# The value projection of two attention groups as seven products each, with strided operands and a weight sum made by an adding transfer

## The chip, the cores and the metric

One core of a Trainium2 chip runs the kernel. The metric is the device time of one execution in microseconds (us); several executions are timed and their median is given. The core has a matrix engine (TensorE, PE in the rows; its loads of a stationary tile are PEld), VectorE (DVE), ScalarE (ACT), GpSimd (POOL) and SyncE (SP). Each runs its own queue of instructions in order, and they wait for each other through semaphores.

## What is computed

The reference is a stack of four transformer layers on 512 tokens of width 1024 in fp32. The change concerns the value part of one of them, a dilated attention with three groups:

```python
proj = (u @ w_in).astype(jnp.float32).reshape(B, S, N_GROUPS, 3, ATT_HEADS, ATT_HEAD_DIM)
for gi, (window, dilation) in enumerate(((128, 1), (512, 4), (2048, 16))):
    q = apply_partial_rope(proj[:, :, gi, 0], cos, sin) * scale
    k = apply_partial_rope(proj[:, :, gi, 1], cos, sin)
    v = proj[:, :, gi, 2]
    o_g, lse_g = dilated_group_attention(q, k, v, window, dilation)
```

For each group `v` is a product of `u` (512 x 1024) with 1024 columns of weights. Groups 1 and 2 use their tokens by residue modulo four, so their rows of `v` are wanted with the tokens of one residue together.

## The kernel before

Matrix products are taken in fp32 precision from two fp32r parts: every operand is split into an upper part (`u_hi`, `w_hi`) and a lower part (`u_lo`, `w_lo`), and three matmuls (`PASSES`: hi x hi, hi x lo, lo x hi) stand for one.

Weights go through the kernel in chunks of 512 rows by 512 columns (four row tiles of 128), numbered in one sequence over the whole kernel. There are three slots (`SLOTS`), so chunk c lies in slot c modulo 3. SyncE loads a chunk into `raw` once chunk c - 3 has been used (`wait_used`, then `chunk`). ScalarE makes its upper part (`split` in its block, line 745), VectorE its lower part (`split` in its block, line 1440), TensorE waits for that with `s_lo`. Both splits run two chunks ahead: while chunk c is being used, `split(name, b, s)` handles c + 2. Each engine's program is a fixed list over `order`, so an instruction that waits holds back everything behind it on its engine.

The value projection is the stage `at_v`: six blocks of 512 weight columns, two chunks each, 96 matmuls of 512 columns a block. In each the stationary tile is 128 tokens of `u` (128 columns) and the moving one is the weights. Block 0 is done in two halves, since it begins while the operand `u` is still being made (`head`, line 2554; lines 1707, 909 and 1719 make the operand from the normed rows, the last of them the lower parts). The blocks of groups 1 and 2 (2 to 5) use copies of `u_hi` and `u_lo` in which the tokens lie by residue; ScalarE (line 1368) and VectorE (line 2267) make these copies during block 1. ScalarE moves each finished tile out of PSUM (line 1363). After the stage VectorE and ScalarE make the tables of the rotary embedding (`rope_tables`). Then the projection of queries and keys follows (`at_qk0`, TensorE's line 2412), whose chunks come in four transfers of 256 KB each.

Late in the kernel, the second product of a feed-forward network is already done as seven products instead of eight, a Strassen-Winograd scheme on 2 x 2 quarters (stages `ff_st`, function `products`, line 2365). Its order of products is A11, A11_21, A2_SUM, A12, A22_21, A22, A_SUM, its weight quarters are loaded by `quadrant_loads` (line 636) in eight transfers of 512 KB, VectorE makes the weight sums (lines 1446, 1455, 1461) and one sum is made by GpSimd's adding transfer (line 724):

```python
pool.wait_ge(s_wsum, 3 * q + 2)
pool.wait_ge(s_lo, c0 + B21 + 1)
pool.dma_start(W21, W11, accum_op=ALU.add).then_inc(s_fourth, 16)
```

VectorE adds each product into the result (`products_added`, line 1478), behind the split of the chunk two further on.

Of the kernel before, what the change touches and what calls it, by code (L numbers as in the profile page):

```python
# [21 lines left out]
P = 128  # L22
S = 512
# [23 lines left out]

A11, A11_21, A12, A22, A22_21, A2_SUM, A_SUM = range(7)
# [96 lines left out]
def gemm_plan():  # L145
# [17 lines left out]
    add("at_v", 6, KT, "act")  # L163
# [15 lines left out]
    c = t = inner = groups = 0  # L179
    freed = {"act": 4, "dve": 4}  # L180
    for name in order:
        g = plan[name]
        if g["evictor"] is None:
            g.update(c0=c, group=groups)
            c += g["chunks"]
            groups += 1
            continue
# [8 lines left out]
def build(nc, a, out, gates, where1, where2, where3, stop=None):  # L196
# [12 lines left out]
    with ctx:  # L209
# [37 lines left out]
        with ExitStack() as room:  # L247
            at_v = sb("at_v", [P, TB, GROUPS * D], F32, room)
            with ExitStack() as sub:
                by_residue_hi, by_residue_lo = sb("u_hi_by_residue", [P, KT, S], F32R, sub), sb("u_lo_by_residue", [P, 4, S], F32R, sub)  # L250
            at_qk = sb("at_qk", [P, 2, 2 * GROUPS, S], F32, room)
# [61 lines left out]
        s_con1, s_cols, s_rows, s_x = sem("constants_and_rope_tables_landed"), sem("columns_landed"), sem("rows_landed"), sem("x_and_masks_landed")  # L313
# [23 lines left out]
        by_residue_lo = [(by_residue_lo if k < 4 else by_residue_in_tmp)[:, k, :] for k in range(KT)]  # L337
        residues = lambda t: t.rearrange("p (c r) -> p r c", r=4)
        by_four = lambda t: t.rearrange("p (r c) -> p r c", r=4)
        s_res_hi, s_res_lo = sem("u_hi_by_residue_ready"), sem("u_lo_by_residue_ready")  # L340
        s_rope1, s_out = sem("first_rope_done"), sem("result_written")
        s_quad = [sem("weights_landed_11_22"), sem("weights_landed_12_21")]
        s_fourth, fourth0 = s_ada[0], 16 * (2 * ADA_BLOCKS - ADA_FIRST)
# [209 lines left out]
        def wait_used(eng, c):  # L553
# [3 lines left out]
            if g["evictor"] is None:  # L557
                eng.wait_ge(s_prod, 14 * g["group"] + 2 * s + 2)
# [54 lines left out]
        def _(sp):  # L613
# [23 lines left out]

            sp.dma_start(con1[:, :], a["con1"]).then_inc(s_con1, 16)
# [16 lines left out]
            for name in order:  # L655
# [16 lines left out]
                if g["evictor"] is None:  # L672
                    continue
# [16 lines left out]
            last = 14 * plan[order[-1]]["group"]  # L690
# [8 lines left out]
        def _(pool):  # L699
# [18 lines left out]
            for name in order:  # L718
                if plan[name]["evictor"] is None:
                    q, c0 = plan[name]["group"], plan[name]["c0"]  # L720

                    pool.wait_ge(s_wsum, 3 * q + 2)
# [5 lines left out]
        def _(act):  # L728
# [3 lines left out]
            def split(name, b, s):  # L732
# [6 lines left out]
                of, _, i = where_chunk[c]  # L739
                if plan[of]["evictor"] is None:  # L740
# [5 lines left out]

            def weights_upper(c, q, i):

                wait_used(act, c - SLOTS)
                if i in (B11, B22, B21):  # L750
                    act.wait_ge(s_quad[1 if i == B21 else 0], 64 * (q + 1))
                elif i == B_SUM4:
                    act.wait_ge(s_fourth, fourth0 + 16 * (q + 1))
                else:
                    act.wait_ge(s_wsum, 3 * q + 1 + (B12_22, B_SUM3, B11_12).index(i))
# [579 lines left out]
            for name in order:  # L1335
# [23 lines left out]
                elif name == "at_v":  # L1359
# [5 lines left out]
                    def upper_by_residue(b):  # L1365
                        if b == 0:
                            for k in range(KT):
                                sc.copy(by_four(by_residue_hi[:, k, :]), residues(u_hi[:, k, :])).then_inc(s_res_hi, 1)
                        if b == 2:
                            gate_rows_out(2, 3)  # L1370
                    linear(name, values, after=upper_by_residue)
# [46 lines left out]
        def _(dve):  # L1418
# [9 lines left out]
            def split(name, b, s):  # L1428
# [5 lines left out]
                of, _, i = where_chunk[c]  # L1434
                if plan[of]["evictor"] is None:
# [5 lines left out]

            def first_sum(q):

                for j in range(2):
                    dve.wait_ge(s_quad[j], 64 * (q + 1))
                tt(W12, W12, W22, ALU.add).then_inc(s_wsum, 1)

            def weights_lower(c, q, i):

                if i == B12_22:  # L1450
                    if q not in FIRST_GROUPS:
                        first_sum(q)
                    dve.wait_ge(s_wsum, 3 * q + 1)
# [4 lines left out]
                if i == B21:  # L1458
                    dve.wait_ge(s_lo, c + 1)
                    dve.wait_ge(s_wsum, 3 * q + 2)  # L1460
                    tt(W12, W11, W22, ALU.subtract).then_inc(s_wsum, 1)

            def products_added(name):
# [5 lines left out]
                for s in range(len(PRODUCTS)):  # L1469
                    if s:  # L1470
                        split(name, 0, s)
                    for t in range(2):
                        dve.wait_ge(s_prod, 14 * q + 2 * s + t + 1)
# [1590 lines left out]
```

## Time and profile before

| what | value |
|---|---|
| median of 3 runs | 2894.68 us (2894.61 to 2895.87) |
| the profiled execution, its own time | 2896.12 us |
| its span in the profile | 2894.3 us |
| TensorE busy with matmuls | 2864.8 us, 99% |
| TensorE busy with weight loads | 2366.1 us, 82% |
| VectorE busy | 1693.6 us, 59% |
| ScalarE busy | 1227.6 us, 42% |
| granted clock, mean | 0.999 |

The span is the time from the first to the last instruction of the profiled execution; the device time has a little around it. Positions in the trace are in us from the start of the span. A matmul's shown duration includes the time in which it fills and drains, so matmuls overlap; what one of them costs in a stream is the distance between two starts.

### The profile page before, as it was taken

Reading aid. Unit: us, or ns where it says so; the run is one execution under the profiler, and the core shown is the slowest. Engines: PE = TensorE matmul, PEld = TensorE weight load, DVE = VectorE, ACT = ScalarE, POOL = GpSimd, SP = SyncE. Lnnn points to the kernel's source line nnn. Section 1 sums busy time; section 2 is a strip of 40 time slices with the busy share of each in tenths; the row PEclk is TensorE's granted clock in tenths of the full one; section 3 lists DMA queues with packets and bytes.
Section 4 is the critical chain, followed back from the end, with each engine's and each line's share of the span. In section 5 each row is a group of like instructions: output and inputs, shape, how many; then the busy total and the mean of one; then the engine's idle time right before and its main releaser. Section 6 shows DMA issues by size and latency. Waiting matters only on the chain.

```text
span 2894.3 us, 38609 instructions
## 1 busy us (share of the span) xinstructions
PE 2864.8 (99%) x16106; PEld 2366.1 (82%) x16106; DVE 1693.6 (59%) x2470; ACT 1227.6 (42%) x1882; POOL 74.0 (3%) x63
## 2 busy tenths in 40 slices
PE   7999999999999999999999999999999999999999
PEld 6878887888887777888888877888888877888887
DVE  6776656645255656533335764666674663656677
ACT  5555422235233333531324465454444455444444
POOL 0000011200000000000000000000000000000000
PEclk9999999999999999999999999999999999999999
DMA  8443355542332222233332222224423222234323
GB/s 303 168 138 117 117 187 184 189 135 91 99 102 65 78 68 77 67 109 95 102 99 84 88 88 74 88 102 131 131 77 106 77 84 73 88 117 131 104 87 115
DMA packets 224637, 320.93 MB, mean 111 GB/s; under 512 B 16496, under 2 KB 123344, under 8 KB 223568
## 3 DMA queue, kind: packets, MB, share of 16 engines
q1 hardware_dynamic: 207504, 266.96, 28.7%
q0 software_dynamic: 11888, 49.29, 5.4%
q10 hardware_dynamic: 5072, 2.23, 0.3%
q8 instruction: 127, 2.08, 0.3%
q14 instruction: 46, 0.38, 0.0%
HBM read 308.98 MB, written 2.11 MB: 107 GB/s over the span
## 4 chain that ended last, share of the span: by engine, by line
PE 89%; DVE 5%; ACT 3%; DMA 2%; issue 1%; ACTq 0%; SPq 0%; DVEq 0%
PE G L2412 46%; PE G L2419 16%; PE G L2471 5%; PE G L2365 4%; PE G L2454 4%; PE X L2365 4%; PE X L2738 1%; PE G L2437 1%; PE X L2516 1%; DMA ada_raw<-in_ada_w 1%; PE X L2752 1%; DVE w_lo L1440 1%; DVE w_lo L1457 1%; DMA raw<-in_w_ff 1%; PE X L2838 1%
## 5 line engine op out<-in xcount | busy, mean ns | idle before, releaser
L2412 PE MATMUL G<-u_hi,w_hi 128*128 128x512 f32 x2096 | 835.0, 398 | 1.9 <-issue 1.9
L2412 PE MATMUL G<-u_hi,w_lo 128*128 128x512 f32 x2096 | 817.6, 390 | 0.0
L2412 PE MATMUL G<-u_lo,w_hi 128*128 128x512 f32 x2096 | 817.0, 390 | 0.0
L1440 DVE TENSOR_TENSOR w_lo<-raw,w_hi 128x2048 fp32r<-128x2048 f32 (+3 forms) x210 | 471.8, 2249 | 437.8 <-ACT w_hi L745 436.7
L745 ACT CAST w_hi<-raw 128x2048 fp32r<-128x2048 f32 (+3 forms) x214 | 401.8, 1878 | 426.1 <-DMA raw<-in_w_ff 148.2
L2412 PEld LDWEIGHTS G<-u_hi,w_hi 128*128 128x128 f32 x2096 | 393.7, 188 | 89.1 <-issue 9.3
L2412 PEld LDWEIGHTS G<-u_hi,w_lo 128*128 128x128 f32 x2096 | 393.5, 188 | 84.1
L2412 PEld LDWEIGHTS G<-u_lo,w_hi 128*128 128x128 f32 x2096 | 394.1, 188 | 78.6 <-issue 1.4
L2252 DVE TENSOR_TENSOR hid_f<-silu_g,G 128x512 f32<-128x512 f32 x44 | 30.1, 688 | 167.2 <-PE G L2412 153.9
L1573 DVE SCALAR_TENSOR_TENSOR acc<-ada_raw,cond,acc 128x512 f32<-128x512 f32 x140 | 105.2, 752 | 13.3 <-DMA ada_raw<-in_ada_w 3.9
L2454 PE MATMUL G<-u_hi,w_hi 128*128 128x256 f32 x384 | 109.3, 285 | 2.8 <-DVE u_lo L1719 2.8
L2454 PE MATMUL G<-u_lo,w_hi 128*128 128x256 f32 x384 | 108.7, 283 | 0.0
L2454 PE MATMUL G<-u_hi,w_lo 128*128 128x256 f32 x384 | 108.6, 283 | 0.0
L2419 PE MATMUL G<-w_hi,hid_hi 128*128 128x512 f32 x256 | 99.7, 389 | 0.6 <-issue 0.6
L2419 PE MATMUL G<-w_lo,hid_hi 128*128 128x512 f32 x256 | 99.6, 389 | 0.0
L2419 PE MATMUL G<-w_hi,hid_lo 128*128 128x512 f32 x256 | 99.6, 389 | 0.0
L2419 PE MATMUL G<-w_hi,u_hi 128*128 128x512 f32 (+1 forms) x256 | 98.2, 384 | 0.0
L2419 PE MATMUL G<-w_lo,u_hi 128*128 128x512 f32 (+1 forms) x256 | 96.5, 377 | 0.0
L2419 PE MATMUL G<-w_hi,u_lo 128*128 128x512 f32 (+1 forms) x256 | 96.4, 377 | 0.0
L1346 ACT ACTIVATE silu_g<-G 128x512 f32<-128x512 f32 x44 | 26.1, 598 | 161.4 <-PE G L2412 152.0
L2365 PE MATMUL G<-w_hi,hidden_sums_hi 128*128 128x512 f32 x224 | 87.2, 389 | 0.0
L2365 PE MATMUL G<-w_hi,hidden_sums_lo 128*128 128x512 f32 x224 | 87.2, 389 | 0.0
(512 smaller groups left out, 4726.3 us busy)
## 6 DMA issues: line engine op xcount, KB each, us to landing
raw<-in_ffn_w_in SPq DMA_DIRECT2D x88, 512.0 KB, 4.8
ada_raw<-in_ada_w POOLq DMA_DIRECT2D x40, 1024.0 KB, 5.7
raw<-in_w_ff SPq DMA_DIRECT2D x72, 512.0 KB, 4.5
raw<-in_w_in SPq DMA_DIRECT2D x56, 512.0 KB, 4.0
raw<-in_attn_w_in SPq DMA_DIRECT2D x96, 256.0 KB, 3.7
raw<-in_ffn_w_out SPq DMA_DIRECT2D x40, 512.0 KB, 4.6
raw<-in_hgrn_w_in SPq DMA_DIRECT2D x32, 512.0 KB, 4.8
yT<-in_w_ff SPq DMA_DIRECT2D x28, 512.0 KB, 8.9
```

The source lines that it names most:

```text
L745: sc.copy(w_hi[slot][:, 0:nk, 0:w], raw[slot][:, 0:nk, 0:w]).then_inc(s_hi, 1)
L1440: tt(w_lo[slot][:, 0:nk, 0:w], raw[slot][:, 0:nk, 0:w], w_hi[slot][:, 0:nk, 0:w].bitcast(F32), ALU.subtract).then_inc(s_lo, 1)
L1457: tt(w_lo[c % SLOTS][:, :, :], weights_of[i], w_hi[c % SLOTS][:, :, :].bitcast(F32), ALU.subtract).then_inc(s_lo, 1)
L1573: ins = stt(acc, ada_raw[:, s, k, :], c, acc, ALU.mult, ALU.add)
L2252: evicted(g, b, 2 + m, lambda: tt(fold(hid_f[:, m, :]), fold(silu_g[:, m, :]), summed_tile(name, b, 2 + m), ALU.mult))
L2365: ins = mm(product_bank(s, t), xs[ix][:, x, k, blk(t)], w[iw][:, k, :], start=s not in order_in_bank and (k, iw, ix) == (0, 0, 0), stop=(k ...
L2412: ins = mm(G[0:c1_ - c0, m, :], w[iw][:, k, c0:c1_], xs[ix][:, x0(b) + kk, :], start=first, stop=last, skip_group_check=True)
L2419: ins = mm(G[:, m, o0:o1], x[:, blk(tok)], w[iw][:, k, c0:c1_], start=first, stop=last, skip_group_check=True)
L2437: ins = mm(G[:, m, :], w[iw][:, k, blk(m)], xs[ix][:, x0(b) + k, :], start=(k, iw, ix) == (0, 0, 0), stop=(k, iw, ix) == (3, 1, 0), skip_g ...
L2454: ins = mm(half_tile(hf, m), w[iw][:, k, m * P:m * P + P], xs[ix][:, kk, half[hf]], start=m % 2 == 0 and kk == 0 and (iw, ix) == (0, 0), s ...
L2471: ins = mm(G[:, j, :], xs[ix][:, kk, blk(j)], w[iw][:, k, :], start=kk == 0 and (iw, ix) == (0, 0), stop=kk == g["ktiles"] - 1 and (iw, ix ...
L2516: ins = tr(turned(k)[:, blk(i)], y[:, 2 * hf + i, blk(k)], ident)
```

## The change

The stage `at_v` keeps two blocks (group 0). Groups 1 and 2 become the stages `at_st0` and `at_st1`, each of seven products. Each product is a 256-token half by a 512-row half of `u` with a 512 x 512 quarter of the weights or a sum of quarters: 2 token tiles x 4 row tiles x 3 passes. The token halves are residues 0 and 1, and residues 2 and 3. Three operands (A11, A12, A22) are read from `u_hi` and `u_lo` with a stride of four tokens; four are sums. Of these VectorE makes the fp32 values (`value_sums`, eight instructions of 1,024 elements a partition), ScalarE the upper parts (`value_sums_upper`) and VectorE the lower parts (`value_sum_lower`). The copies by residue go.

The weight quarters live in the rooms `V11`, `V12` and `V22`; `V12` holds B12, then B21. They are loaded by SyncE (`value_quadrant`, `value_loads`), the first three ahead of the second chunk of block 1. B_SUM4 is made by GpSimd's adding transfer of `V11` onto `V12`; after it VectorE takes `V22` from `V11` for B11_12. The order of products is A11, A11_21, A2_SUM, A12, A22, A22_21, A_SUM, numbered here from 0. Products 0 and 3 are moved out by ScalarE, the others are added or subtracted by VectorE.

```diff
-    add("at_v", 6, KT, "act")
+    add("at_v", 2, KT, "act")
+    for i in range(2):
+        add(f"at_st{i}", 1, KT, None)
...
+        V11, V12, V22 = yT[:, 0:4, :], yT[:, 4:8, :], tmp[:, 0:4, :]
+        value_weights = {B11: V11, B12_22: V12, B_SUM3: V11, B21: V12, B_SUM4: V12, B11_12: V11, B22: V22}
+        VALUE_PRODUCTS, VALUE_WEIGHTS = (A11, A11_21, A2_SUM, A12, A22, A22_21, A_SUM), (B11, B12_22, B_SUM3, B21, B_SUM4, B11_12, B22)
+        by_residue = lambda t, kh, th: t.rearrange("p k (c r) -> p k r c", r=4)[:, 4 * kh:4 * kh + 4, 2 * th:2 * th + 2, :]
...
+            def value_loads(name):
+
+                i, c0 = int(name[-1]), plan[name]["c0"]
+                sp.wait_ge(s_lo, c0 + 2)
+                value_quadrant(i, V12, 1, 0, s_quad[1])
+                if i == 0:
+                    sp.wait_ge(s_lo, c0 + 5)
+                    value_quadrant(1, V12, 0, 1, s_quad[1])
+                    sp.wait_ge(s_lo, c0 + 6)
+                    value_quadrant(1, V11, 0, 0, s_quad[0])
+                    sp.wait_ge(s_lo, c0 + 7)
+                    value_quadrant(1, V22, 1, 1, s_v22)
...
+                        if name == "at_v" and (b, s) == (1, 1):
+
+                            sp.wait_ge(s_u, 6 * KT)
+                            value_quadrant(0, V12, 0, 1, s_quad[1])
+                            value_quadrant(0, V22, 1, 1, s_v22)
+                            value_quadrant(0, V11, 0, 0, s_quad[0])
...
+                if name.startswith("at_st"):
+                    pool.wait_ge(s_wsum, 3 * int(name[-1]) + 2)
+                    pool.wait_ge(s_lo, plan[name]["c0"] + 4)
+                    pool.dma_start(V12, V11, accum_op=ALU.add).then_inc(s_fourth, 16)
...
+            def value_weights_lower(c, q, s):
+
+                x = VALUE_WEIGHTS[s]
+                if x == B12_22:
+                    if q:
+                        first_value_sum(q)
+                    dve.wait_ge(s_wsum, 3 * q + 1)
+                    dve.wait_ge(s_lo, c)
+                    tt(V11, V11, V12, ALU.add).then_inc(s_wsum, 1)
+                elif x == B_SUM4:
+                    dve.wait_ge(s_fourth, fourth0 + 16 * (q + 1))
+                    tt(V11, V11, V22, ALU.subtract).then_inc(s_wsum, 1)
+                dve.wait_ge(s_hi, c + 1)
+                tt(w_lo[c % SLOTS][:, :, :], value_weights[x], w_hi[c % SLOTS][:, :, :].bitcast(F32), ALU.subtract).then_inc(s_lo, 1)
...
+            def value_products_added(name):
+
+                g, i = plan[name], int(name[-1])
+                first, second = (slice((i + 1) * D + 512 * nh, (i + 1) * D + 512 * nh + 512) for nh in range(2))
+                for s in range(len(PRODUCTS)):
+                    split(name, 0, s)
+                    if s in (0, 3):
+                        continue
+                    for t in range(2):
...
                 elif name == "at_v":
...
+                    split(name, 0, 0)
+                    split(name, 0, 1)
+                    first_value_sum(0)
+                    value_sums()
+                    split(name, 1, 0)
+                    value_sum_lower(A11_21, 1)
+                    value_sum_lower(A2_SUM, 0)
+                    split(name, 1, 1)
+                    value_sum_lower(A22_21, 3)
+                    value_sum_lower(A_SUM, 2)
...
+            def value_products(name):
+
+                g, i = plan[name], int(name[-1])
+                for s, x in enumerate(VALUE_PRODUCTS):
+                    pe.wait_ge(s_lo, g["c0"] + s + 1)
+                    slot = (g["c0"] + s) % SLOTS
+                    w, xs = (w_hi[slot], w_lo[slot]), value_operands[x]
+                    if x in VALUE_READY:
+                        pe.wait_ge(s_res_lo, VALUE_READY[x])
+                    for t in range(2):
+                        bank = (G[:, t, :], G[:, 2 + t, :], X[:, t, :], G[:, t, :], G[:, 2 + t, :], X[:, t, :], X[:, t, :])[s]
+                        added = {1: -6 + t + 1, 2: -2 + t + 1, 4: t + 1, 5: 2 + t + 1, 6: 6 + t + 1}.get(s)
...
```

The feed-forward groups keep their work; only the values that their semaphores are counted up to move.

## Rows read from the trace of the kernel before

**Rows 1.** The chain of waits, 690 to 860: start, length, what, matmuls

```profile
699.26 108.80 PE G L2419 x480
808.06 48.96 PE G L2412 x216
```

**Rows 2.** Timeline of VectorE, 676 to 722: start, duration, what, idle before

```profile
692.11 0.42 DVE L1719 TENSOR_TENSOR u_lo<-tmp,u_hi 128x256 fp32r<-128x256 f32 x1 [0.21 <-ACT u_hi L909]
...
701.72 2.29 DVE L1440 TENSOR_TENSOR w_lo<-raw,w_hi 128x2048 fp32r<-128x2048 f32 x1 [5.58 <-ACT w_hi L745]
703.93 2.24 DVE L2267 CAST u_lo_by_residue<-u_lo 128x512 fp32r<-128x512 f32 x4
```

**Rows 3.** Weight loads by line: count, minimum/median/maximum ns, first and last start

```profile
L2738 PEld LDWEIGHTS X<-at_qk x768: 134/138/167, 856.9 to 1168.5; 128*32 128x32 f32 x192
...
L2749 PEld LDWEIGHTS X<-at_v,tmp x512: 101/107/133, 867.4 to 1173.7; 32*32 32x32 f32 x43, 96*32 96x32 f32 x43, 128*32 128x32 f32 x43, 64*32 64x32 f32 x42
...
L2419 PEld LDWEIGHTS G<-w_hi,u_hi_by_residue x128: 187/188/188, 720.6 to 807.0; 128*128 128x128 f32 x128
```

**Rows 4.** Timeline, 1008 to 1012: four packed weight loads in a row

```profile
1010.94 0.52 PEld L2752 LDWEIGHTS X<-at_v,tmp 128*128 128x128 f32 x4 [0.20 <-issue]
```

**Rows 5.** Timeline of ScalarE, 1895 to 1990

```profile
1925.83 1.91 ACT L745 CAST w_hi<-raw 128x2048 fp32r<-128x2048 f32 x1 [0.73 <-DMA raw<-in_w_ff]
...
1967.00 1.91 ACT L756 CAST w_hi<-yT 128x2048 fp32r<-128x2048 f32 x1 [3.34 <-DMA yT<-yT]
...
1977.45 1.91 ACT L745 CAST w_hi<-raw 128x2048 fp32r<-128x2048 f32 x1 [6.72 <-DMA raw<-in_w_ff]
```

**Rows 6.** Groups of VectorE by shape, 690 to 2000: count, busy us, mean ns

```profile
L1633 DVE TENSOR_TENSOR w_lo<-raw,w_hi 128x1024 fp32r<-128x1024 f32 x4 | 4.9, 1216 | 0.0
```

**Rows 7.** Timeline of VectorE, 1895 to 1990

```profile
1957.05 2.28 DVE L1457 TENSOR_TENSOR w_lo<-yT,w_hi 128x2048 fp32r<-128x2048 f32 x1
...
1979.39 2.29 DVE L1440 TENSOR_TENSOR w_lo<-raw,w_hi 128x2048 fp32r<-128x2048 f32 x1 [3.56 <-ACT w_hi L745]
1981.60 1.28 DVE L1478 TENSOR_TENSOR h_by_token<-h_by_token,G 128x512 f32<-128x512 f32 x2
```

**Rows 8.** Timeline of GpSimd, 1880 to 1990

```profile
1959.94 0.93 POOL L724 DMA_DIRECT2D yT<-yT  x1 [1354.10 <-DVE w_lo L1457]
```

**Rows 9.** Timeline of SyncE's transfers, 780 to 830

```profile
786.33 43.89 SPq L621 DMA_DIRECT2D raw<-in_attn_w_in  x17
```

**Rows 10.** Timeline of ScalarE, 783 to 850

```profile
792.73 1.91 ACT L745 CAST w_hi<-raw 128x2048 fp32r<-128x2048 f32 x1 [4.00 <-DMA raw<-in_attn_w_in]
```

**Rows 11.** Timeline of SyncE's transfers, 1880 to 1990

```profile
1907.80 0.88 SPq L636 DMA_DIRECT2D yT<-in_w_ff  x2
...
1916.48 67.71 SPq L625 DMA_DIRECT2D raw<-in_w_ff  x8
```

**Rows 12.** The chain of waits, 1935 to 2000

```profile
1972.41 5.44 PE G L2365 x24
1977.85 5.44 PE X L2365 x24
```

**Rows 13.** Busy us and instructions by stretch, then clock, DMA share, GB/s

```profile
25.00:28.00 3.00, 1.21 (x11) 0.97 (x10) 1.63 (x5) 2.23 (x4) 0.00 (x0) 1.00 1.05 387
28.00:31.00 3.00, 2.80 (x7) 2.25 (x8) 2.46 (x3) 2.97 (x5) 0.00 (x0) 0.57 1.05 387
...
474.00:477.00 3.00, 1.29 (x6) 1.11 (x7) 2.96 (x6) 1.68 (x1) 1.89 (x1) 1.00 0.90 331
```

**Rows 14.** Copies by line: count, minimum/median/maximum ns, first and last start

```profile
L1368 ACT CAST u_hi_by_residue<-u_hi x8: 1118/1124/1132, 701.6 to 708.7; 128x512 fp32r<-128x512 f32 x8
...
L2267 DVE CAST u_lo_by_residue<-u_lo x4: 630/634/644, 703.9 to 705.5; 128x512 fp32r<-128x512 f32 x4
...
L1363 ACT COPY at_v<-G x24: 577/587/593, 693.7 to 808.1; 128x512 f32<-128x512 f32 x24
```

More of the change, by code:

```diff
@@ L183, in gemm_plan @@
         if g["evictor"] is None:
-            g.update(c0=c, group=groups)
+            g.update(c0=c, prod0=prod0, add0=add0)
             c += g["chunks"]
-            groups += 1
+            prod0 += 14
+            if name.startswith("at_st"):
+                g.update(act0=freed["act"])
+                freed["act"] += 4
+                add0 += 10
+            else:
+                g.update(group=groups)
+                groups += 1
+                add0 += 14
             continue
@@ L689, in _ @@
             by_token = out[0].rearrange("(b p) n -> p b n", p=P)
-            last = 14 * plan[order[-1]]["group"]
+            last = plan[order[-1]]["add0"]
             for added, rows, cols in ((10, slice(2, 4), upper_columns), (12, slice(0, 4), lower_columns), (13, slice(0, 1), upper_columns),
@@ L745, in split, with value_weights_upper, value_products_out @@
                 sc.copy(w_hi[slot][:, 0:nk, 0:w], raw[slot][:, 0:nk, 0:w]).then_inc(s_hi, 1)
+            def value_weights_upper(c, q, s):
+                wait_used(act, c - SLOTS)
+                x = VALUE_WEIGHTS[s]
+                if x == B11:
+                    act.wait_ge(s_quad[0], 32 * (q + 1))
+                elif x == B21:
+                    act.wait_ge(s_quad[1], 64 * (q + 1))
+                elif x == B22:
+                    act.wait_ge(s_v22, v22_0 + 32 * (q + 1))
+                elif x == B_SUM4:
+                    act.wait_ge(s_fourth, fourth0 + 16 * (q + 1))
+                else:
+                    act.wait_ge(s_wsum, 3 * q + 1 + (B12_22, B_SUM3, B11_12).index(x))
+                sc.copy(w_hi[c % SLOTS][:, :, :], value_weights[x]).then_inc(s_hi, 1)
+            def value_products_out(name):
+                g, i = plan[name], int(name[-1])
[4 more added lines that the diff above has]
+                        for t in range(2):
+                            act.wait_ge(s_prod, g["prod0"] + 2 * s + t + 1)
+                            if s == 0:
+                                sc.copy(at_v[:, 2 + t, first], G[:, t, :])
+                                ins = sc.activation(at_v[:, t, second], G[:, t, :], ACT.Identity, scale=-1.0)
+                            else:
+                                ins = sc.copy(at_v[:, t, first], G[:, t, :])
+                            ins.then_inc(s_free["act"], 1)
             def weights_upper(c, q, i):
@@ new lines, in value_sums @@
+            def value_sums():
+                hi = lambda kh, th: by_residue(u_hi, kh, th).bitcast(F32)
+                lo = lambda kh, th: by_residue(u_lo, kh, th).bitcast(F32)
+                f11_s2, f21_t1, f12_s4, f22_s1 = value_f
+                n.own(s_u)
+                tt(f11_s2, hi(0, 0), lo(0, 0), ALU.add)
+                tt(f21_t1, hi(0, 1), lo(0, 1), ALU.add)
+                link(tt(f22_s1, hi(1, 1), lo(1, 1), ALU.add))
+                link(tt(f22_s1, f22_s1, f21_t1, ALU.subtract))
+                n.give(tt(f21_t1, f11_s2, f21_t1, ALU.subtract), d2a)
+                ins = stt(f11_s2, f22_s1, -1.0, f11_s2, ALU.mult, ALU.subtract)
+                n.give(ins, d2a)
+                n.own(d2a)
+                link(tt(f12_s4, hi(1, 0), lo(1, 0), ALU.add))
+                n.give(stt(f12_s4, f11_s2, -1.0, f12_s4, ALU.mult, ALU.subtract), d2a)
@@ L2568, in head @@
                                 turn(tail_of[name], 1)
[L2570 removed]
+            after_products = {order[i + 1]: plan[name]["add0"] for i, name in enumerate(order[:-1]) if plan[name]["evictor"] is None}
             tail_of = {b: a_ for a_, b in TAILS.items()}
```

155 lines of the change are left out of this document (113 added, 42 removed).

## Prediction

> **What bounds the kernel now.** Read the chain of waits first. From 699.26 on it is one run of 480 matmuls of line 2419 in 108.80 us, followed without a gap by the projection after it [rows 1]: 226.7 ns a matmul, whatever the other engines do. In the value projection TensorE alone sets the time. VectorE there is idle most of the time, each of its weight subtractions ending a wait for ScalarE [rows 2]. So removed matmuls come back in full, at 0.2267 us each, but only while every weight operand is made before its product begins. That cover is what I read next: the order of the queues and what each step costs.
>
> **The gain.** Four blocks of 96 matmuls (384) become two groups of 7 products x 24 (336). 48 x 0.2267 = 10.9 us less. No later stage changes its work, so what moves is the start of the query and key projection, 808.06 now [rows 1].
>
> **Strided operands on TensorE.** Three products of seven take their stationary tile from every fourth token: 2 x 3 x 24 = 144 loads. The trace has such a load only 32 columns wide: 138 ns against 107 ns for a packed one, so 31 ns per 32 columns. At 128 columns that is 188 + 4 x 31 = 312 ns [rows 3]. The matmul does not wait for the whole of a load: four packed loads in a row take 0.52 us with the last one's 0.19, so 0.11 us each, though one lasts 0.19 [rows 4]. A strided one then needs 0.110 + 0.124 = 0.234 us, against a pitch of 0.227. Bounds: nothing, or 312 - 227 = 85 ns if nothing of the excess overlaps, 0 to 12.2 us over 144. I take 7 ns, 1.0 us, since the packed row shows the overlap.
> The Trainium skill (SBUF — State Buffer, Specifications (TRN2)) says that full bandwidth needs at least two accesses in the same 16-byte line, and that each crossing pays. Fp32 with a stride of four crosses at every element. The trace agrees for the stationary load (138 against 107 ns) and for ScalarE; for VectorE see the rivals.
>
> **Prices of the chain.** ScalarE's upper part of a chunk: 1.9 us [rows 5]. VectorE's lower part or weight sum: 2.2 us from start to start [rows 2]. A sum of 1,024 elements: 1.22, next start after 1.13 [rows 6]. Adding a product: 0.64 each [rows 7]. The adding transfer: VectorE's lower part starts at 1957.05 and ends at 1959.3 [rows 7], GpSimd issues at 1959.94 [rows 8], ScalarE is released at 1967.00 [rows 5]: 7.65 us from end to use. Two weight transfers, 1 MB, in an empty queue: a feed-forward product ends at 1972.41 [rows 12], which lets SyncE issue, and ScalarE is released at 1977.45 [rows 5], 5.04; with the waits 5.1 us. The first half chunk of the next projection (four transfers): issue 786.33 [rows 9], release 792.73 [rows 10], 6.4 us.
>
> **Block 1 of the value projection.** Its second chunk used to be ready at 701.72 + 2.2 = 703.9 [rows 2]; TensorE needs it 432 matmuls ahead of 808.06 [rows 1], at 710.1. Now SyncE first waits for the whole operand (last lower part 692.11 + 0.42 = 692.5 [rows 2]) and issues six 512 KB transfers ahead of the chunk's two. The nearest row: eight such and two more, issued from 1907.80 on [rows 11], release ScalarE at 1925.83 [rows 5], 18.0 us for ten. Less two at 1.3 us (0.39 MB per us): 15.4 us, so 708.0. Upper 1.9, lower 2.2: 712.15. **Stall 2.1 us**; the block ends at 723.0 instead of 721.0. Bounds: none if the chunk lands by 705.6, 4 us if ten transfers' time is needed.
>
> **First group, seven products of 5.44 us** (24 x 0.2267; the strided ones 5.61).
> - Product 0. Behind the late chunk VectorE has in order: the first weight sum (2.2), eight operand sums (8 x 1.13 and about 0.5 for waits on itself, 9.5), then the lower part of B11 (2.2). 712.1 + 13.9 = 726.1. The block ended at 723.0: **stall 3.1**. ScalarE's evictions, behind its casts of these sums, end at about 725.2, under this.
> - Product 1. Two lower parts of operand sums (2.3), the weight sum (2.2), the lower part of B12_22 (2.2): 732.8. Product 0 ends at 731.7: **stall 1.1**.
> - Products 2 and 3 are covered: 737.2 and 742.0 against 738.3 and 743.7.
> - Product 4 needs B_SUM4. B21 can be loaded only after 732.8, into the room of B12: + 5.1 + 1.9 + 2.2 = 742.0. Then the adding transfer 7.65, VectorE's V11 - V22 (2.2), the lower part (2.2): 754.1. Product 3 ends at 749.3: **stall 4.8**. The feed-forward groups take their fourth sum one product later and into a buffer of its own; here one product of cover less is 5.4 us less.
> - Product 6 accumulates in the bank of product 5 and waits for VectorE to have added that. VectorE first serves the split for the next group: B11 of group 2 is loaded after the lower part of B11_12 (754.1, two adds 1.2, 2.2: 757.5): + 5.1 + 1.9 + 2.2 = 766.8, and the add 0.64: 767.5. Product 5 ends at 765.2: **stall 2.3**. It ends at 772.9.
>
> **Second group.** V22 reloads behind the lower part of B22 (759.7) and has landed when VectorE comes to it, behind the adds of product 5, at 768.1. Two weight sums and the lower part of B12_22, 6.6: 774.7, in time for product 1 (778.6). B21, + 9.2 and a wait: 784.0. Adding transfer and two VectorE steps: 796.0, product 3 ends at 795.1: **stall 1.0**. Product 4 ends at 801.7. SyncE's queue holds the first chunk of the next projection behind that end, as its room counter is three chunks back: + 6.4 + 1.9 + 2.2 = 812.2, and VectorE adds product 5 only after it: 812.9. Product 5 ended at 807.1: **stall 5.7**. A feed-forward group shows the same order: its fifth product ends at 1972.41 [rows 12], ScalarE is released at 1977.45 [rows 5], VectorE splits at 1979.39 and adds product 5 at 1981.60 [rows 7], 3.7 us after product 6 began at 1977.85 [rows 12]. There nobody waits for the add; here product 6 does.
>
> **The clock.** It fell to a mean of 0.57 in 28 to 31 (part of it at 1.2 GHz), after three us with TensorE busy 1.21; it stayed at 1.00 after 1.29 of three around 475 [rows 13]. Stalls of 4.8 and 5.7 us leave it less than either. Matmuls then took 2.80 / 7 = 0.40 us [rows 13]; some eight so are 1.5 us. After product 4 this hides behind VectorE's late add; after the last stall it is paid. I take + 1.5.
>
> **Sum.** Stalls 2.1 + 3.1 + 1.1 + 4.8 + 2.3 + 1.0 + 5.7 = 20.1. -10.9 + 1.0 + 20.1 + 1.5 = **+11.7 us**. The removed copies by residue (eight on ScalarE, eight on VectorE [rows 14]) were beside TensorE's work and give nothing. The rope tables move behind the last add; they take some 6 us and are wanted some 13 us into the next stage, nothing. The profiled execution took 2896.12 us, its span 2894.3, the median of the runs is 2894.68: so a span near 2906.0, a profiled execution near 2907.8, a median near **2906.4**.
>
> **Rivals.**
> - A, the forecast: the stalls as above, 2901 to 2910.
> - B, strides cost more. ScalarE's strided copy of 512 took 1124 ns, its packed one 587; VectorE's strided copy 634 for 512 elements, which is the pace of a packed sum, 1216 for 1,024 [rows 6, 14]; so I leave VectorE's sums at that pace. If a VectorE sum with two strided operands goes at half pace as ScalarE does, four sums cost 1.1 us more each: + 4.3, 2910.7. If the 85 ns are paid, part hides under the stalls: about + 4.6, 2911. The skill's rule on 16-byte lines, named above, asks for just this on VectorE too.
> - C, the weights arrive sooner. The chunk at 705.5 takes 2.5 us off the first chain (stalls in block 1 and before product 0), each 1 MB in 4.5 us takes 0.6 off the stalls before products 4 and 6 of both groups, 2.4, and the last load of four transfers at 5.4 us one more: about -6, 2900.5 and below, within 0.2%.
> - D, faster: the cover holds. Of the feed-forward products shown both run on at 5.44 us [rows 12], with the same three engines and sums. If the operands are made ahead here too, what is left is -10.9 + 1.0 = -9.9: 2884.8. It decides from stalls under 4.1 us in all. Against it stands that the load of B21, the adding transfer and two VectorE steps alone come to 21 us after B12_22, against three products, 16.5.
>
> **Chances.** What a measurement tells from no change is 0.2%, 5.8 us. A 0.55, B 0.22, both slower; other slower cases 0.02; C 0.14, within; D 0.07, faster. Slower 0.79, same 0.14, faster 0.07. Range 2898 to 2912: it takes in A, most of B and the upper part of C. A's own is 2901 to 2910.
>
> **What the profile after would show.** TensorE's gaps: about 2 us in the middle of block 1, 3 before product 0, 5 before the first group's product 4, 2 and 6 before the two last products; ScalarE or VectorE idle on the adding transfer for some 7 us twice; strided loads of about 312 ns with a pitch of 0.23 to 0.24; next projection starting near 820. Wrong if the pitch of strided products is over 0.25, if the chunk of block 1 lands before 706, or if product 6 does not wait for the add of product 5.

## The result, and the profile after

The changed kernel takes 2915.45 us (median of 4 runs, 2914.24 to 2917.35), the kernel before 2894.64 in the runs beside it. The ratio is 1.0072, 95% interval 1.0055 to 1.0089. It is slower by 20.8 us; 11.7 were forecast, and the range ended at 2912. The direction and the mechanism were right, the size was not. The profiled execution took 2914.24 us, its span is 2912.4.

From the first matmul of block 1 (696.77) to the first of the next projection (824.75) are 127.98 us, against 108.80 before [rows 1]: 19.2 more. The two profiled executions differ ahead of this too, where the change does nothing. Block 1 begins 2.3 us earlier here (its first matmul stood at 699.09 before, at the edge of the chain's piece of 699.26 in [rows 1]): 1.2 of that is there by 472 us, and 1.1 is a shorter pause of TensorE near 473 (1.2 us from start to start, 2.3 before). From the next projection to the end it is 1.2 us more.

The chain of waits in the changed kernel, from the first group's reload of B21 on:

```profile
731.63 0.37 SPq L664
732.04 7.14 DMA yT<-in_attn_w_in
739.26 1.92 ACT w_hi L817
741.20 2.30 DVE w_lo L1569
743.54 0.56 issue
744.10 6.97 DMA yT<-yT
751.10 2.29 DVE yT L1567
753.39 2.21 DVE w_lo L1569
755.65 8.21 PE G L2547 x24
763.86 5.46 PE X L2547 x24
...
804.90 0.37 SPq L642
...
806.41 5.16 DMA raw<-in_attn_w_in
811.59 1.91 ACT w_hi L801
...
815.73 0.69 DVE at_v L1612
816.56 8.36 PE X L2547 x24
824.91 5.21 PE G L2617 x23
```

Before, this stretch was nothing but TensorE. Now a load, ScalarE, VectorE, an adding transfer and VectorE twice set the start of product 4 (755.65), and a load and VectorE's late add that of the last product (816.56). Both products take over 8 us where 24 matmuls take 5.46 with nothing ahead of them. That is the clock. Busy time by stretch in the changed kernel (PE, PEld, DVE, ACT, POOL, then granted clock, DMA share, GB/s):

```profile
718.00:725.00 7.00, 1.17 (x7) 0.63 (x5) 6.93 (x6) 5.29 (x7) 0.00 (x0) 0.87 0.13 1
725.00:728.00 3.00, 3.00 (x7) 2.46 (x8) 3.00 (x3) 2.55 (x3) 0.00 (x0) 0.50 0.02 0
749.00:755.00 6.00, 0.70 (x4) 0.38 (x2) 3.90 (x2) 3.42 (x2) 0.00 (x0) 0.91 0.22 44
755.00:758.00 3.00, 2.35 (x6) 1.92 (x7) 3.00 (x4) 3.00 (x4) 0.00 (x0) 0.50 0.37 69
797.00:799.00 2.00, 0.42 (x3) 0.16 (x1) 2.00 (x2) 2.00 (x3) 0.00 (x0) 1.00 0.00 0
816.00:819.00 3.00, 2.44 (x6) 1.99 (x7) 1.84 (x3) 2.75 (x2) 0.00 (x0) 0.50 0.00 0
819.00:822.00 3.00, 3.00 (x9) 2.32 (x8) 1.46 (x1) 0.43 (x1) 0.00 (x0) 0.50 0.00 0
```

Behind each wait of some 6 us the granted clock is 0.50, the 1.2 GHz level; after the short wait near 797 it stays at 1.00. The lowest of the rows of before was 0.57 [rows 13].

VectorE in the changed kernel, from the second chunk of block 1 to the operand of product 0 (start, duration):

```profile
705.59 2.29 DVE L1548 TENSOR_TENSOR w_lo<-raw,w_hi 128x2048 fp32r<-128x2048 f32 x1 [11.77 <-ACT w_hi L801]
707.80 2.28 DVE L1554 TENSOR_TENSOR yT<-yT,tmp 128x2048 f32<-128x2048 f32 x1
710.00 1.97 DVE L1577 TENSOR_TENSOR at_v<-u_hi,u_lo 128x1024 f32<-128x1024 f32 x1
...
715.77 1.23 DVE L1580 TENSOR_TENSOR at_v<-at_v 128x1024 f32<-128x1024 f32 x1
...
722.64 2.29 DVE L1569 TENSOR_TENSOR w_lo<-yT,w_hi 128x2048 fp32r<-128x2048 f32 x1
```

The four sums with two strided operands take 1.96 to 2.04 us, the packed ones 1.23. Product 0 begins at 724.98, the moment the last row shown is done, 6.2 us after the last matmul of block 1 at 718.76.

All instructions of the seven products' line: weight loads strided and packed (count, minimum/median/maximum ns), then what TensorE was idle for (us, times; the idle time of matmuls and of weight loads is added up here, so it is about twice the gaps):

```profile
L2547 PEld LDWEIGHTS G<-w_hi,u_hi x48: 308/310/335, 725.0 to 803.8; 128*128 128x128 f32 x48
...
L2547 PEld LDWEIGHTS X<-w_hi,value_sums_hi x32: 187/188/190, 738.2 to 809.3; 128*128 128x128 f32 x32
...
  DVE w_lo L1569: 27.8, 6
...
  DVE at_v L1612: 6.2, 1
```

The distance between the 433 starts from 696.77 to 824.75 gives the account of the stage:

| term | forecast | measured |
|---|---|---|
| 48 matmuls fewer | -10.9 | -10.9 |
| strided loads, 144 | +1.0 | +1.2 (start to start 0.235) |
| waits | +20.1 | +20.2 in four gaps |
| matmuls at the lower clock | +1.5 | +7.7 (37 intervals, most of them 0.43) |
| small waits, and the rest | 0 | +0.9 |
| sum | +11.7 | +19.2 |

The row of the lower clock holds the intervals that begin while the granted clock is 0.50, less the usual step. The first of each of the three stretches took 0.57 to 0.61 us. Behind a gap with the clock at 1.00 it took 0.47 (798.84), so some 0.7 us of the 7.7 are an estimate of what the three gaps would have cost at full clock too.

### The profile page after: what moved, and what is told of

Same layout as the page of the kernel before. It is cut to its first block, busy times and chain, and to the rows that moved or that the text cites. A ratio compares the mean times of both kernels' runs of the same rounds, so it can differ in the third digit from the quotient of the medians.

```text
span 2912.4 us, 38589 instructions
## 1 busy us (share of the span) xinstructions
PE 2863.8 (98%) x16054; PEld 2366.6 (81%) x16058; DVE 1744.6 (60%) x2506; ACT 1231.8 (42%) x1880; POOL 75.7 (3%) x65
## 4 chain that ended last, share of the span: by engine, by line
PE 88%; DVE 5%; ACT 3%; DMA 2%; issue 1%; SPq 0%; ACTq 0%; DVEq 0%; POOLq 0%
PE G L2617 47%; PE G L2622 13%; PE G L2674 5%; PE G L2657 4%; PE G L2570 4%; PE X L2570 3%; PE X L2941 1%; DMA yT<-yT 1%; PE G L2640 1%; PE X L2719 1%; PE G L2547 1%; PE X L2547 1%; PE X L2955 1%; PE X L3041 1%; PE X L3051 1%
## 5 line engine op out<-in xcount | busy, mean ns | idle before, releaser
L1548 DVE TENSOR_TENSOR w_lo<-raw,w_hi 128x2048 fp32r<-128x2048 f32 (+3 forms) x202 | 453.5, 2247 | 383.0 <-ACT w_hi L801 382.0
L801 ACT CAST w_hi<-raw 128x2048 fp32r<-128x2048 f32 (+3 forms) x206 | 386.4, 1877 | 432.7 <-DMA raw<-in_w_ff 150.8
```

Of the source, the lines that this page charges most:

```text
L801: sc.copy(w_hi[slot][:, 0:nk, 0:w], raw[slot][:, 0:nk, 0:w]).then_inc(s_hi, 1)
L1548: tt(w_lo[slot][:, 0:nk, 0:w], raw[slot][:, 0:nk, 0:w], w_hi[slot][:, 0:nk, 0:w].bitcast(F32), ALU.subtract).then_inc(s_lo, 1)
```

## The experiments

The stage column is from the first matmul of block 1 to the first of the next projection in the profiled execution; the gaps are those of TensorE of over 0.9 us within it, each less the 0.227 of a usual step. The last column counts the matmuls of the stage that begin while the granted clock is 0.50. These three columns are of one execution each, which can lie up to 3.6 us off its kernel's median. In the text a gap is given from start to start.

| kernel | median us | ratio, interval | stage us | gaps us | matmuls at 1.2 GHz |
|---|---|---|---|---|---|
| before | 2894.6 to 2895.4 | | 108.8 | 0 | 0 |
| changed | 2915.45 | 1.0072 (1.0055 to 1.0089) | 128.0 | 20.2 | 37 |
| adds first | 2910.64 | 1.0052 (1.0037 to 1.0067) | 123.2 | 17.1 | 33 |
| fourth sum by VectorE | 2909.50 | 1.0051 (1.0036 to 1.0066) | 122.5 | 17.0 | 27 |
| gaps filled | 2911.05 | 1.0054 (1.0039 to 1.0069) | 123.9 | 9.0 | 0 |
| packed operands | 2909.07 | 1.0051 (1.0034 to 1.0068) | 122.1 | 17.3 | 27 |
| gate rows later | 2911.46 | 1.0059 (1.0045 to 1.0073) | 124.9 | 19.5 | 25 |
| adds first, fourth sum | 2898.08 | 1.0012 (1.0003 to 1.0021) | 109.7 | 7.4 | 13 |
| adds first, sums later | 2904.80 | 1.0035 (1.0021 to 1.0049) | 116.5 | 12.6 | 14 |
| three edits | 2898.21 | 1.0010 (1.0001 to 1.0019) | 107.2 | 4.9 | 7 |
| gate rows between loads | 2895.06 | 1.0000 (0.9991 to 1.0009) | 107.3 | 4.9 | 8 |
| last sum later | 2891.10 | 0.9983 (0.9974 to 0.9993) | 103.8 | 3.0 | 0 |

The first four edits ran beside each other, so did the next four, and the last two, each set with the kernel before. The gaps filled leave out the matmuls added there.

**Product 5 added ahead of the split** (adds first).

```diff
 for s in range(len(PRODUCTS)):
-    split(name, 0, s)
+    if s != 5:
+        split(name, 0, s)
...
         ins.then_inc(s_add, 1)
+    if s == 5:
+        split(name, 0, s)
```

> Edit: in both groups VectorE adds product 5 before it splits the chunk two further on, not after; all else as in the changed kernel. Theory (stalls plus the half clock behind them): the gap of 6.4 us before product 6 of the second group and the slow matmuls behind it, 2.9 us, go, so about 9 us less than the changed kernel, near 2906 us; the gap of 6.2 us before product 0 and that of 6.1 us before the first group's product 4 stay. Rival (the late load of the next projection's chunk is the cost, whoever waits for it): TensorE stops for it at the start of the next projection instead, with a gap of 4 us or more there, and at most 4 us are saved, 2911 us or more.

It took 2910.64, 4.8 less than the changed kernel, where the theory had 9 and the rival at most 4. Product 6 no longer waits for the add of product 5, and the next projection follows without a gap. So the rival's stop at its start did not come. But the gap ahead of the second group's product 4 rose from 2.0 to 5.5 us, and the clock fell there instead. The add was the place of the wait; the chain of the weights stood right behind it.

**The fourth weight sum by VectorE** in place of the adding transfer.

```diff
-    pool.dma_start(V12, V11, accum_op=ALU.add).then_inc(s_fourth, 16)
...
 elif x == B_SUM4:
-    dve.wait_ge(s_fourth, fourth0 + 16 * (q + 1))
+    dve.wait_ge(s_lo, c)
+    tt(V12, V12, V11, ALU.add).then_inc(s_wsum, 1)
+    dve.wait_ge(s_wsum, 4 * q + 3)
     tt(V11, V11, V22, ALU.subtract).then_inc(s_wsum, 1)
```

> Edit: the fourth weight sum of either group is made by VectorE (2.2 us) in place of the adding transfer (7.6 us from the end of the lower part to its use); all else as in the changed kernel. Theory: the chain to product 4 is 5.4 us shorter twice. The first group's gap of 6.1 us falls to about 2 us and the clock stays up behind it (2.6 us more), the second group's 1.7 us goes; but product 6 of the first group then waits some 4 us for the late weights B11 behind which VectorE adds product 5. Together 3 to 6 us less, 2909.5 to 2912.5 us. Rival (the transfer lies beside other work and only the load of B21 counts): gap before product 4 unchanged, within 1 us of 2915.5.

2909.5, 5.9 less, within the expected 3 to 6. The gap ahead of the first group's product 4 fell from 6.3 to 2.0 us with the clock kept; 3.7 came back ahead of product 6, with 8 matmuls at the lower clock, and a gap of 5.9 ahead of the last product stayed.

**Gaps filled with matmuls** that nobody reads, so that TensorE stays busy.

```diff
 for s, x in enumerate(VALUE_PRODUCTS):
+    if (i, s) in ((0, 0), (0, 4), (1, 6)):
+        for _ in range(20):
+            mm(X[:, 3, :], u_hi[:, 0, 0:P], u_hi[:, 0, :], start=True, stop=True, skip_group_check=True)
     pe.wait_ge(s_lo, g["c0"] + s + 1)
```

> Edit: TensorE does 20 matmuls of u by u (512 columns, 4.5 us) into an unused bank before it waits for product 0 and product 4 of the first group and for product 6 of the second; all else as in the changed kernel. Their sums are read by nobody. Theory (the half clock is the price of the idle gaps): the gaps shrink to under 2 us, the matmuls behind them take 0.227 and 0.235 us from the first on, the granted clock is 1.00 there, and some 8 us are saved, near 2907.5 us, with the next products starting no earlier than now. Rival (the matmuls behind the gaps are slow for another reason, such as their strided loads): nothing changes, 2915 us or a little more.

2911.05: 4.4 less, not 8. The clock was held through the whole stage, as these stretches show in the places of the two first long gaps (columns as above):

```profile
721.00:727.00 6.00, 5.03 (x23) 3.82 (x21) 5.93 (x4) 4.57 (x6) 0.00 (x0) 1.00 0.10 1
...
751.00:758.00 7.00, 5.00 (x22) 3.79 (x21) 4.39 (x2) 3.93 (x3) 0.00 (x0) 1.00 0.20 40
```

So the low clock was worth 4.4 us net, of the 7.7 in the account above. Part of the rest had been cover: while TensorE was slow, the other engines gained on it, and with the clock held they were late in more places (1.0 us ahead of product 1, 2.4 ahead of the first product 6). The 60 matmuls added take 13.6 us at 0.227 each; with the gaps of 9.0 that is 22.6 us, against 20.2 in the changed kernel.

**Packed operands.** `by_residue` takes 128 tokens that lie together instead of every fourth, for TensorE and VectorE both; groups 1 and 2 thus compute the values of other tokens.

```diff
-by_residue = lambda t, kh, th: t.rearrange("p k (c r) -> p k r c", r=4)[:, 4 * kh:4 * kh + 4, 2 * th:2 * th + 2, :]
+by_residue = lambda t, kh, th: t.rearrange("p k (r c) -> p k r c", r=4)[:, 4 * kh:4 * kh + 4, 2 * th:2 * th + 2, :]
```

> Edit: the operands and VectorE's sums take 256 neighbouring tokens in place of the tokens of two residues, so that nothing is strided; the values of groups 1 and 2 then belong to other tokens than the reference's, the work is the same in number. Theory (strides cost little, waits much): the four sums fall from 1.97 to 1.23 us, 3.0 us off the gap before product 0, and 72 to 144 matmuls go from 0.235 to 0.227 us, 0.6 to 1.2 us: some 4 us less, 2911.5 us; 2.5 us more if the gap of 3 us that is left keeps the clock up. Rival (the strides are the main cost of the change): 10 us less or more, 2905 us or under.

2909.07, 6.4 less, against 10 or more by the rival. The theory had some 4, and 2.5 more if the gap of 3 us kept the clock up. The clock did fall behind that gap (8 matmuls), but for a shorter time than before. In the stage, 5.9 us shorter, the gaps give 2.9, the lower clock 2.3 and the strided steps 1.0. VectorE's sum and a weight load of the same operand, in this kernel:

```profile
711.36 1.22 DVE L1577 TENSOR_TENSOR at_v<-u_hi,u_lo 128x1024 f32<-128x1024 f32 x1
```
```profile
L2547 PEld LDWEIGHTS G<-w_hi,u_lo x48: 187/188/338, 723.4 to 801.4; 128*128 128x128 f32 x48
```

The sums fell from 1.97 to 1.22 us, the loads from 310 to 188 ns, and the gap ahead of product 0 from 6.2 to 3.2, which is the four sums' 3.0. So rival B was half true: VectorE pays for the stride, TensorE hardly does, since its 122 ns more a load became 8 ns a step.

**Gate rows later.** ScalarE's two transfers `gates<-mix` move from the end of block 1 to behind the rope tables.

```diff
             evicted(g, 1, m, lambda: sc.copy(at_v[:, m, 512:1024], G[:, m, :]))
-        gate_rows_out(2, 3)
...
         n.give(sc.activation(cosT[:, :], tmp[:, 3, :], ACT.Sin, scale=-1.0, bias=float(np.pi / 2)), a2d)
+        gate_rows_out(2, 3)
```

> The changed kernel with ScalarE's two transfers of gate rows (gates<-mix, many small elements) moved from the end of block 1 to behind the rope tables. In the changed kernel they were under way from 722.9 to 735.2 us while the first group's reload of B21 (1 MB) took 7.6 us from SyncE's issue to ScalarE's use; the second group's took 5.0 with nothing beside it. Theory: the small elements slow the load. Then the first group's load falls to about 5.1 us, the gap ahead of product 4 from 6.3 to about 4 us, with fewer matmuls at the lower clock behind it: 2.5 to 4 us less than the changed kernel, 2911.5 to 2913. Rival: the load is slow for another reason (its distance behind other traffic); the gap stays at 6 us, time 2915.

2911.46, 4.0 less, as the theory had it. The chain of waits there:

```profile
731.70 0.37 SPq L664
...
732.11 4.70 DMA yT<-in_attn_w_in
...
736.89 1.92 ACT w_hi L817
```

From issue to use it is 5.2 us, against 7.6 with the gate rows under way, and the gap ahead of product 4 fell from 6.3 to 4.2. A gap of 2.6 us came ahead of product 6.

**Both first edits together.** No further line is changed.

> The two single edits measured before, in one kernel: product 5 is added ahead of the next chunk's split (alone 4.8 us less, 2910.6), and B_SUM4 is made by VectorE in place of the adding transfer (alone 5.9 less, 2909.5). Each alone left a gap of about 6 us in the second group that the other one removes. Theory: they add up or do better, 2915.4 - 10.7 = 2904.7, or 2903 when the last low-clock stretch (2.5 us) goes too; the only gap of about 6 us left is the one ahead of product 0. Rival: the pressure is one chain, and what is won in one place is waited for at the next: 2907 to 2909.

2898.08: 17.4 less, where the two alone gave 10.7. Only the gap ahead of product 0 (6.3) and one of 1.6 ahead of product 4 are left, and the second group has none. The theory counted too little, and the rival expected less than the sum where it was more. Each edit alone left a wait of over 5 us in the second group, with its stretch at the lower clock, that the other one took away.

**Adds first, operand sums later.** VectorE splits B11 ahead of the first weight sum. `value_sums` is cut in three parts: the first makes A11_21 and the fp32 half of A22, the second A2_SUM and A22_21, the third A_SUM, and ScalarE's upper parts move with them. The gate rows go out behind the rope tables.

```diff
-first_value_sum(0)
-value_sums()
 split(name, 1, 0)
-value_sum_lower(A11_21, 1)
-value_sum_lower(A2_SUM, 0)
+first_value_sum(0)
+value_sums(0)
+value_sum_lower(A11_21, 2)
 split(name, 1, 1)
-value_sum_lower(A22_21, 3)
-value_sum_lower(A_SUM, 2)
+value_sums(1)
...
+    if (i, s) == (0, 0):
+        value_sum_lower(A2_SUM, 0)
+    elif (i, s) == (0, 3):
+        value_sum_lower(A22_21, 3)
+        value_sums(2)
+        value_sum_lower(A_SUM, 2)
```

> Product 5 added ahead of the next chunk's split, and the order of VectorE's queue around block 1 changed: the second chunk of block 1 keeps its place, then the split of B11 and only the operand sums that product 1 needs; the sums for A22_21 and A_SUM follow behind products 0 and 3. The adding transfer stays; the gate rows go out behind the rope tables. It is to be compared with the kernel that only adds first (2910.6). Theory: the 6.2 us gap ahead of product 0 is VectorE's queue of sums, so it shrinks to under 1 us with its stretch at the lower clock, but the chain of weights (B21, adding transfer) is now the next to be late, as it starts only a few us sooner: about 5 us less, 2905.5. Rival: the whole 8 us come back, 2902.5, or, if the sums only move the wait to product 1 and product 3, none, 2910.

2904.8, 5.8 under the kernel that only adds first. The gap ahead of product 0 is gone, and 5.9 us stand ahead of product 4, where the adding transfer is now late; 5.0 stand ahead of the second group's product 4. Behind the stage a new gap of 3.9 us appeared (840.09); the next kernel shows what it is.

**The three edits**: adds first, fourth sum by VectorE, operand sums later.

> All edits: product 5 added ahead of the split, B_SUM4 by VectorE, operand sums spread behind products, gate rows later. Theory (the stage lost its gain to stalls and to the clock behind them, and to nothing else): gap ahead of product 0 under 1 us, gaps ahead of products 4 and 6 of both groups at most 2 us each, no matmuls at the lower clock; sum of the terms left -10.9 + 1.2 for the strided loads + about 6 of stalls, so 2889 to 2894, below the kernel before by up to 0.2%. Rival: the reload of B21 into the room of B12 is the bound whatever VectorE's order (load 5.1 + upper 1.9 + lower 2.2 + the fourth sum and two further steps against two products): 2897 to 2902, still slower than before.

2898.21 (2893.44 to 2902.86), above the 2889 to 2894 of the theory. It lies where the rival put it, 2897 to 2902, but not for the rival's reason: the gap ahead of product 4, which the reload of B21 leads to, is 1.6 us. Ahead of product 6 there are 3.7 us, with 7 matmuls at the lower clock, where the theory had at most 2 and none. The stage is 107.2, less than before the change, but the next one lost: there is a gap of 1.9 us at 831. The profiled execution took 2895.25, 3.0 less than the median; where the other executions lost the difference stays open. The chain of waits there, and then the transfers by queue from 814 to 832 in the same kernel:

```profile
816.82 13.81 DMA raw<-in_attn_w_in
830.63 0.02 issue
830.65 1.90 ACT w_hi L797
```
```profile
DMA  0000037999999969999999996997963720632689
GB/s 0 0 0 0 0 105 203 306 322 250 212 271 68 7 7 5 11 21 18 16 19 22 64 34 38 62 40 32 92 75 40 45 7 16 114 41 35 73 208 305
...
q1 hardware_dynamic: 2859, 1.42, 64.9%
q10 hardware_dynamic: 2080, 0.01, 40.5%
...
gates<-mix ACTq DMA_DIRECT2D x2, 4.0 KB, 12.7
```

The gate rows are 0.01 MB in 2080 packets. With loads beside them the transfer engines are busy at 5 to 22 GB/s for some 4 us, and the last of four 256 KB loads takes 13.8 us, where such a one took 5.16 in the changed kernel's chain above.
The Trainium skill (DMA: Bandwidth & Descriptors, Specifications) asks for transfers of at least 512 bytes for full rate; these packets have some 4 bytes, and the trace agrees: with no load beside them they moved at 5 to 6 GB/s (gate rows between loads, near 706 us).

**Gate rows between the loads**: directly behind ScalarE's upper part of B11, with no load until 725.

```diff
 linear(name, values, bs=range(1))
 split(name, 1, 0)
+gate_rows_out(2, 3)
...
-        gate_rows_out(2, 3)
```

> The kernel with all edits, but the gate rows go out right behind ScalarE's upper part of B11 in block 1 (near 708 us), in a stretch without loads until B21 is asked for at 725, in place of behind the rope tables. There, in the kernel with all edits, they began at 816.1 us, beside four loads of 256 KB of the next projection, of which the last took 13.8 us from SyncE's issue to ScalarE's use, and TensorE waited (gap 1.9 us, eight matmuls at the lower clock before it in the stage). Theory: gate rows and loads slow each other, so with nothing beside them both go at their own pace: the next stage is 1.5 to 3 us shorter, the time 2895 to 2896.5. Rival: the loads are late there for another reason; the gap at 831 us stays, 2898. If the gate rows last into the load of B21, that load is longer than 5.2 us and the gap ahead of product 4 grows from 1.6 us to 4.

2895.06, 3.2 less than the kernel with three edits, as expected. The two ratios to before overlap within their intervals (1.0001 to 1.0019, 0.9991 to 1.0009), so the times alone do not settle it. The trace does for the gap: the transfers began at 704.6, nothing waited for them, and the gap in the next stage is gone. In the stage itself nothing changed.

**The last sum behind product 4.** A_SUM is made one product later, behind the lower part of B22.

```diff
     elif (i, s) == (0, 3):
         value_sum_lower(A22_21, 3)
-        value_sums(2)
-        value_sum_lower(A_SUM, 2)
+    elif (i, s) == (0, 4):
+        value_sums(2)
...
         ins.then_inc(s_add, 1)
+    if (i, s) == (0, 4):
+        value_sum_lower(A_SUM, 2)
```

> As the kernel with the gate rows between loads, and the two operations that make A_SUM, with its parts, moved behind VectorE's split of the chunk of product 5's follower, so that they do not stand ahead of B22's lower part and of the adds of products 4 and 5. In the kernel with all edits VectorE is busy nearly without a gap from 705 to 762 us and product 6 began 3.7 us late (758.37), behind the add of product 5 at 757.54. Theory: the first group is bound by VectorE's queue and its order decides: product 6 begins 1.5 to 2.5 us sooner and keeps the full clock (another 1 to 1.5 us), so 2892 to 2894, about 0.1% under the kernel before. Rival: VectorE's work is the bound whatever its order, and the wait moves to A_SUM's lower part or to the second group's first products: no change from the kernel beside it, 2895 to 2896.5.

2891.10, 4.0 less again, and 4.3 under the kernel before (0.9974 to 0.9993), a little more than expected. The gap ahead of product 6 fell from 3.7 to 1.8 us and the clock no longer falls. Its chain of waits, and its stretches (columns as above):

```profile
757.54 5.73 PE X L2554 x24
763.27 11.09 PE G L2554 x48
774.36 5.45 PE X L2554 x24
779.80 11.28 PE G L2554 x48
791.08 10.89 PE X L2554 x48
801.97 28.11 PE G L2624 x124
```
```profile
720.00:742.00 22.00, 21.61 (x93) 19.08 (x92) 19.43 (x13) 10.12 (x10) 0.00 (x0) 1.00 0.15 48
742.00:758.00 16.00, 13.37 (x56) 11.71 (x56) 15.97 (x15) 7.59 (x7) 0.00 (x0) 1.00 0.60 198
758.00:801.80 43.80, 43.80 (x192) 39.10 (x191) 33.12 (x22) 16.44 (x13) 0.00 (x0) 1.00 0.25 71
```

The second group has no wait at all. In the first VectorE is busy 15.97 of 16 us from 742 to 758: there the seven products make more work for it than fits beside them, and the gap ahead of product 6 stands in it. The other one left, 1.6 us ahead of product 4, is at the end of a chain that also passes through ScalarE, whose upper part of B21 begins at 732.53 behind casts and evictions. What the stage gains is 5.0 us of the 9.9 that rival D gave it.

Loading the next projection's first chunk ahead of product 4 was not tried: its room in `raw` is also that of a lower part still in use.

## Why the prediction was right in direction and wrong in size

- **Gain of 10.9, and strides on TensorE.** Right. Load 310 ns (312 worked out), step 0.235 (0.234).
- **Block 1, stall 2.1.** Wrong: 0.4 in two short waits. The eight transfers ahead of ScalarE's upper part took 13.4 us from first issue to use (690.24 to 703.64), not 15.4. On before's positions that is 705.9, close to the early landing that rival C named, and one of the forecast's own signs of being wrong (before 706). It gave nothing in the end: the block ended sooner and the wait moved to product 0.
- **Product 0, stall 3.1.** Measured 6.0. I left VectorE's strided sums at the packed pace from a single strided copy; they cost 0.75 us more each, 3.0 in all (packed operands: gap 6.2 to 3.2). The chunk's earlier landing took 2.0 off VectorE's end, and the block ended 1.7 sooner: 3.1 + 3.0 - 2.0 + 1.7 = 5.8. The Trainium skill (SBUF — State Buffer, Specifications (TRN2)) names a penalty for each crossing to a new 16-byte line, and gives no size. For VectorE's sums of two operands with a stride of 16 bytes the trace agrees: 1.97 us against 1.22. The comparison itself was off: the copy's 634 ns [rows 14] were set against a sum of two operands. A packed step of 512 elements with one operand takes 0.42 us in the trace of before (VectorE's timeline, 783 to 850), so the strided copy had already paid:

```profile
812.73 0.42 DVE L1949 CAST tmp<-sinT 128x512 f32<-128x512 int32 x1
```

- **Product 1, stall 1.1.** None. A later product 0 and its slow matmuls gave the cover.
- **Product 4.** 6.1 for 4.8. The load of B21 took 7.6 us, not 5.1: the gate rows, which I did not count among the transfers, were under way when it was issued (gate rows later: 5.2). The adding transfer took 7.6 from end to use, as forecast.
- **Product 6, stall 2.3.** 0.2: slow matmuls in product 4 covered VectorE, as the prediction said they would; with the clock held the gap there was 2.4 (gaps filled).
- **Second group, 1.0 and 5.7.** Measured 1.7 and 6.4, by the order forecast: the lower part at 813.52, the add at 815.73, the product at 816.56.
- **The waits' sum**, 20.1, was measured at 20.2, with errors of both signs that cover each other: a later wait shrinks when an earlier one grows. That the two sums agree so closely is luck.
- **The clock, 1.5.** This is the step that failed: "some eight so are 1.5 us", paid once. The stretch behind product 4 was taken as hidden, and none was counted behind product 0, whose stall was forecast at 3.1; even a gap of 3.2 us there had the clock down for 8 matmuls (packed operands). Three gaps of about 6 us were followed by 12, 12 and 13 matmuls at the lower level, 37 intervals and 7.7 us; net of what they cover 4.4 (gaps filled). Those 6.2 us more, small waits of 0.9 that I did not count, and 0.3 in the strides and the waits' sum are the miss in the stage, 7.5 us, within rounding.
- **Outside the stage.** The medians are 9.1 us further apart than forecast, 1.6 more than the stage's 7.5; behind the stage the profiled execution is 1.2 us longer. In the last feed-forward group the adding transfer took 9.10 us there, with a gap of 1.9 us behind it (2901.63). All kernels of the study but the one with filled gaps have such a gap there, from 1.9 to 2.0 us, and the trace of before has none; what ties it to the change stays open.
- **Rival D**, the cover holds, was not a matter of the load and the adding transfer alone: with the edits above half of its gain is there. Of the rest 3.0 us are the two gaps in the first group, and 1.5 are short waits.

## What to carry to other kernels

When a removed product makes operand sums, count the engine that makes them as its queue orders them, one by one, and ask which of them the next product needs; order, one sum on another engine and the place of two small transfers were worth 24 us here. Price a wait together with the matmuls at half clock behind it, and try coupled waits together: two edits of 5 us each gave 17. Look for small-element transfers beside a load that sets a start.

## What the hardware showed that was not expected

- After each gap of 3.2 to 6.7 us in and right behind this stage TensorE ran 7 to 13 matmuls at the 1.2 GHz level, 0.2 us more each; after those of up to 2.6 us none.
- The length of a gap alone does not tell it. Near 105 us in the kernel with adds first and the fourth sum, a gap of 2.1 us behind 32 matmuls of 32 columns was followed by 10 matmuls at the lower level (107.02 to 110.43). At the same place in the kernel with filled gaps, 2.3 us were followed by none. TensorE was busy 1.12 of the 3 us from 104 to 107 in the first and 0.94 in the second, so the prediction's comparison of such busy times [rows 13] would not have told them apart either.
- A VectorE sum of 1,024 elements with two operands strided by 16 bytes took 1.97 us against 1.22 packed, while its strided copy of 512 elements took 634 ns [rows 14], about what half a packed sum takes, where a packed one took 420.
- Two transfers of 4 KB, together 2080 packets, took 10 to 13 us from issue to landing and lengthened loads issued before they had landed: 1 MB from 5.2 to 7.6 us, the last of four of 256 KB to 13.8 us. In the changed kernel the last of their packets in the trace stands at 725, and that 1 MB was issued at 731.63, so how the ones slow the other stays open.
- With TensorE's clock held by matmuls nobody reads, 4.4 of the 7.7 us of the lower clock came back in the time; waits, the added matmuls counted in, grew by 2.4.
